# Attention in a two-layer mixer and MoE kernel: the values are held in the array, the probabilities stream, two heads share the columns, and the output stays transposed

## What is computed

```
# windowed heads, latent queries: a band of +-128 latent keys, all context keys, one sink
p = softmax(concat([s_loc, s_ctx, s_sink]));  o = p[:, :-1] @ v
# latent-attention heads: all latent and context keys
p = softmax(s * (64 + 32) ** -0.5);           o = p @ v
# context queries (first layer only): context keys alone
y = concat([o_swa, o_gdn, o_mla]) @ w_out
x = x + g1 * rms_norm(y)
h2 = rms_norm(x) * (1 + sc2) + sh2
```

## Time and profile before

| | us |
|---|---|
| median of 3 runs | 3174.64 |
| lowest and highest | 3173.73, 3174.68 |
| profiled execution: its own time | 3172.74 |
| its span (first to last instruction) | 3170.9 |
| mean granted TensorE clock | 0.948 of full |

### The profile page before, as it was taken

How to read it: one execution, slowest core, us unless ns; L and a number is a source line. 1 busy time by engine, 2 the same in 40 slices (tenths; PEclk the granted TensorE clock), 3 DMA queues, 4 the chain that set the end, 5 groups by cost and what they waited for, 6 DMA issues and landing times. The chain is left out here.

```text
span 3170.9 us, 57994 instructions
## 1 busy us (share of the span) xinstructions
PE 2841.6 (90%) x20700; PEld 1444.7 (46%) x20701; DVE 1516.1 (48%) x2944; ACT 840.6 (27%) x1553; POOL 949.0 (30%) x928
## 2 busy tenths in 40 slices
PE   6998897988999999999977998988989898978895
PEld 3654665874543333333323554667854332222232
DVE  2432653864554444444436443636745544433345
ACT  2231543112212222222225232441122222211222
POOL 0020003521035555555531020006231544433440
PEclk8999998999999999999989999999989999988998
DMA  6100530013348999899949200420134699999955
GB/s 245 62 19 8 186 138 21 4 70 130 146 165 295 367 363 369 319 401 394 364 178 374 95 30 8 159 69 3 35 133 170 249 410 414 406 408 413 408 202 244
DMA packets 129436, 671.63 MB, mean 212 GB/s; under 512 B 38296, under 2 KB 56344, under 8 KB 87392
## 3 DMA queue, kind: packets, MB, share of 16 engines
q1 hardware_dynamic: 86400, 569.34, 46.0%
q0 software_dynamic: 38528, 84.02, 7.2%
q10 hardware_dynamic: 4320, 15.73, 1.2%
HBM read 619.64 MB, written 84.93 MB: 222 GB/s over the span
## 5 line engine op out<-in xcount | busy, mean ns | idle before, releaser
L2325 PE MATMUL psum<-arena 128*64 x1792 | 821.0, 612 | 77.1 <-DVE arena L2419 77.1
L2327 PE MATMUL psum<-arena 128*64 128x512 f32 x1792 | 821.0, 612 | 0.0
L2288 POOL DMA_INDIRECT arena<-h,arena x456 | 521.9, 1145 | 410.0 <-DVE arena L1593 285.6
L2325 PEld LDWEIGHTS psum<-arena 128*64 128x64 f32 x1792 | 242.9, 141 | 566.4 <-issue 566.4
L822 PE MATMUL psum<-arena 128*128 128x480 f32 (+3 forms) x1088 | 405.3, 530 | 16.0 <-PEq L167 8.0
L2347 PE MATMUL psum<-arena 128*64 x896 | 407.7, 598 | 13.2 <-DVE arena L2426 13.2
L2349 PE MATMUL psum<-arena 128*64 128x512 f32 x896 | 407.7, 598 | 0.0
L822 PEld LDWEIGHTS psum<-arena 128*128 128x128 f32 x1088 | 209.3, 196 | 190.6 <-issue 178.2
L2375 ACT ACTIVATE arena<-psum 128x256 f32<-128x256 f32 x112 | 42.9, 383 | 901.5 <-PE psum L2327 901.5
L2347 PEld LDWEIGHTS psum<-arena 128*64 128x64 f32 x896 | 123.7, 138 | 271.7 <-issue 271.7
L2327 PEld LDWEIGHTS psum<-arena 128*64 128x64 f32 x1792 | 242.9, 141 | 0.0
(11 more groups left out here) (360 smaller groups left out, 3987.0 us busy)
## 6 DMA issues: line engine op xcount, KB each, us to landing
arena<-in_w_gu SPq DMA_DIRECT2D x130, 2048.0 KB, 16.6
arena<-in_w_dn SPq DMA_DIRECT2D x130, 1024.0 KB, 13.8
arena<-in_ada SPq DMA_DIRECT2D x24, 2048.0 KB, 8.5
arena<-y_routed SPq DMA_DIRECT2D x40, 1024.0 KB, 14.4
arena<-in_w_gdn SPq DMA_DIRECT2D x6, 1536.0 KB, 11.1
arena<-in_w_out SPq DMA_DIRECT2D x2, 4096.0 KB, 14.9
arena<-in_w_tok SPq DMA_DIRECT2D x4, 1920.0 KB, 7.8
arena<-h,arena POOLq DMA_INDIRECT x464, 7.9
```

Source lines behind the costliest of these rows:

```text
L2288: nc.gpsimd.indirect_dma_start(xg[:, u % 2, b], None, h2_quads, bass.IndirectOffsetOnAxis(ap=idx[:, u, b:b + 1], axis=0), bounds_check=QUA ...
L2325: nc.tensor.matmul(psum[half(0), 2 + r, :], xT[:, r, rows_of(k, 0)], W[:, bass.ds(at + k * 2 * DE, 2 * DE)], start=(k == 0), stop=(k == DK ...
L2327: last = nc.tensor.matmul(psum[half(1), 2 + r, :], xT[:, r, rows_of(k, 1)], late_gu[:, k * 2 * DE:(k + 1) * 2 * DE], start=(k == 0), stop= ...
```

## The change

The attention stage is rewritten; the merge follows from its new output.

- Units are ordered by *pairs* of heads: for each pair and query tile, first one head, then the other. Each SWA pair takes a head of either key group; MLA heads pair up in order.
- POOL, which had nothing to do here, multiplies E by the reciprocal of the sum (in place, one instruction to a unit, 256 to 768 columns) before it is turned. E gets 4 buffers instead of 2.
- `turn` runs two units behind the scores (LAG) and now waits for POOL and for the copy of the unit before.
- `values` runs once for 4 units (two pairs): each key tile's 64 value columns are the weights, 128 columns of ET stream; one head of a pair writes PSUM partitions 0 to 63, the other 64 to 127, and the two alternate. Results are head width by queries.
- DVE's four scaled copies of 64 columns become one plain copy of 256 columns to `catT`. Its old `write` per unit is gone.
- `catT` goes to HBM in 5 stores a layer instead of 10. The rows of `w_out` are permuted on the host to the new order of heads.
- In the merge the attention part loads straight into `cT`; only the 3 GDN blocks are turned and copied. As `cT` has two buffers, `load(i)` gets one more wait: until `project(i-2)` is done. The gate's DMA is still the third of `load_cat`.

```diff
-            for h in range(SWA_H + MH):
+            for m, pair in enumerate(PAIRS):
                 for i in range(nq):
+                    for h in pair:
...
+            LAG, RING, GROUP = 2, 4, 4
...
+                    @block.gpsimd
+                    def _(pool):
+                        for u in range(NU):
+                            w = width(units[u])
+                            pool.wait_ge(normed, u + 1)
+                            nc.gpsimd.tensor_scalar(E[:, u % RING, 0:w], E[:, u % RING, 0:w], den[:, u % 4:u % 4 + 1], None, ALU.mult).then_inc(scaled, 1)
...
                         def turn(u):
-                            pe.wait_ge(exp_done, u + 1)
+                            pe.wait_ge(scaled, u + 1)
+                            if u:
+                                pe.wait_ge(et_done, u)
...
-                        def values(u):
+                        def values(g):
+                            pe.wait_ge(et_done, GROUP * (g + 1))
...
+                                for c, kt in enumerate(keys):
+                                    for x, ((h, i, swa, _, _), r) in enumerate(two):
+                                        v = vb[:, kt, ...] if swa else mv[:, kt, h - SWA_H, :]
+                                        last = nc.tensor.matmul(outs(g)[64 * x:64 * x + 64, p * P:(p + 1) * P], v, ET[:, r, c * P:(c + 1) * P],
...
-                            if u:
-                                values(u - 1)
-                            turn(u)
+                            if u >= GROUP + LAG and (u - LAG) % GROUP == 0:
+                                values((u - LAG) // GROUP - 1)
+                            if u >= LAG:
+                                turn(u - LAG)
...
+                        def write(g):
+                            m, i = 2 * g // nq, 2 * g % nq
+                            dve.wait_ge(pv_done, g + 1)
+                            nc.vector.tensor_copy(catT[:, m, i * P:(i + 2) * P], outs(g)).then_inc(out_done, 1)
...
+        def load_cat(sp, i, cT, sz, c_in):
+            for a, b, at in ((0, NBAND, 0), (NBAND, len(PAIRS), NBAND + GH // 2)):
+                sp.dma_start(cT[:, i % 2, ...], catT_dram[a:b, :, i * P:(i + 1) * P]...).then_inc(c_in[i % 2], 16)
             sp.dma_start(sz[:, i % 2], gate_dram[i * P:(i + 1) * P, :]).then_inc(c_in[i % 2], 16)
...
                             if i >= 2:
                                 sp.wait_ge(turned_a, i - 1)
-                                load_cat(sp, i, ct, sz, c_in)
+                                sp.wait_ge(y_prod, i - 1)
+                                load_cat(sp, i, cT, sz, c_in)
...
-                            for k in range(DK):
+                            for k in range(GH // 2):
...
                             pe.wait_ge(cT_ready, i + 1)
+                            pe.wait_ge(c_in[i % 2], 48 * (i // 2) + 48)
```

More of the change, by code:

```diff
@@ L38 @@
 Z_A = 96
+PAIRS = [(j, SWA_H // SWA_KV + j) for j in range(SWA_H // SWA_KV)] + [(SWA_H + 2 * j, SWA_H + 2 * j + 1) for j in range(MH // 2)]
+NBAND = SWA_H // 2
 TOKC = [W_VB + SWA_KV * HD + KVR + MROPE, SWA_H * HD + Z_A, GH * HD - Z_A + QR]
@@ L1025, in _ @@
                         score(0)
-                        for u in range(NU):
+                        for u in range(NU + LAG):
                             n, at = u // EVERY, u % EVERY
@@ L1086, in _ @@
                             bias(u)
-                            if u >= 2:
-                                write(u - 2)
                             if u >= 1:
                                 norm(u - 1)
-                        if NU >= 2:
-                            write(NU - 2)
+                            if u > GROUP + LAG and (u - LAG - 1) % GROUP == 0:
+                                write((u - LAG - 1) // GROUP - 1)
                         norm(NU - 1)
-                        write(NU - 1)
+                        for g in range((NU - 1 - LAG - 1) // GROUP, NU // GROUP):
+                            write(g)
                     @block.scalar
@@ L1112, in _, with take_row @@
                             nc.scalar.copy(kz[64 * g:64 * g + 64, g], skT[64 * g:64 * g + 64, :]).then_inc(kz_ready, 1)
-                        for u in range(min(2, NU)):
+                        def take_row(m):
+                            act.wait_ge(mod_prod, m + 1)
+                            if m:
+                                act.wait_ge(mod_turned, m)
+                            nc.scalar.copy(row[:, :], psum[:, MOD, :]).then_inc(row_ready, 1)
+                        for u in range(LAG + 1):
+                            if u == 2:
+                                take_row(0)
                             exps(u)
@@ L1778, in take_cat @@
                                 act.wait_ge(y_prod, i - 1)
[L1779 removed]
+                            nc.scalar.copy(cT[:, i % 2, NBAND * P:(NBAND + GH // 2) * P], psum[:, 0, 0:GH * HD]).then_inc(cT_ready, 1)
                         def square_y(i):
@@ L2810 @@
     uq = I["mla_w_uq"]
+    head = [h if h < SWA_H else GH + h for pair in PAIRS for h in pair]
+    heads = head[:2 * NBAND] + list(range(SWA_H, SWA_H + GH)) + head[2 * NBAND:]
+    rows_out = (_np.array(heads)[:, None] * HD + _np.arange(HD)[None, :]).reshape(-1)
     arrays = {
```

110 lines of the change are left out of this document (49 added, 61 removed).

## The result

The changed kernel took 3191.66 us (median of 5 runs, 3188.41 to 3195.41) against 3173.73 us (5 runs, 3173.09 to 3174.68): the ratio is 1.0055, 95% interval 1.0043 to 1.0068. That is 18 us slower, outside the forecast's range of 3142 to 3186. The profiled execution is the slowest of the five, 3195.41 with a span of 3193.6 us.

A forecast was written before the change was run, and what follows sets the result against it. The prediction took PE to set the attention stages' pace, values passes being held by their 128-column weight loads. Attention -39 and merge +30 gave -9, so 3165 us; the range leaving out two in ten was 3142 to 3186.

The forecast's parts named there:

- Values on column halves, -51 us: Attention values: two heads' halves run side by side, a key tile costing 0.107 us instead of 0.22, over 448 tiles.
- The change of shape, +6: Attention: TensorE going from halves to the full array and back costs 0.24 us, paid 25 times, +6 us.
- VectorE, ScalarE and the score buffers, +5: Attention: scores wait for exponentials two units back, 16 us if nothing is absorbed, 0 if all is; +5 taken.
- GpSimd, 0: Attention: POOL's multiplication at 1.1 to 2.2 ns a column, 1.5 taken, is hidden up to about 2.6; costs nothing.
- Attention, -39: Both attention stages together: -51 + 6 + 5 + 1 = -39 us, with bounds -56 and -20.
- The merge, +30: Merge of both layers: -1, +21 for five late gates and +10 for the clock, +30 us, bounds 14 to 45.
- The landing: Merge: the gate's load, issued when the projection ends, lands in 3.2 us; the row read gave 3.6.
- The clock: Merge: idle gaps halve TensorE's granted clock for the work behind, 2 us in each of five places, +10.
- Five transposes less: Merge: fewer transposes and copied columns per tile save almost nothing, as PE waits for ACT's copy anyway; -1 us.
- Rival 1: Merge hides its loads better: gate lands in 2.6 us, clock doesn't fall, merge costs 14; 3149 us, chance 0.20.
- Rival 2: Attention paced by DVE and the two score buffers, gaining only 20 us; 3185 us, slower, chance 0.16.
- rivals 3 and 4: Attention: POOL becomes the bound (3203 us), or halves don't overlap at 128 columns (3215 us); together 0.05.

The follow-up runs named there:

- 7: Kernel 1 with the two heads of a pair worked one after the other, each on its column half, instead of alternating by key tile: 3174.97 us.
- 11: Kernel 1 with the values gathered in pairs of units instead of fours, 50 changes to halves and back instead of 25: 3149.04 us.
- 8: Kernel 1 with GpSimd multiplying only 2 columns of each unit, every wait kept, values wrong: 3196.17 us; first layer's attention 171.0 us in both.
- 9: Kernel 1 with GpSimd scaling the first 512 columns of units of 5 and 6 key tiles and VectorE the rest: 3154.04 us.
- 5: The changed kernel with the gate's DMA issued first of the three and counted on semaphores of its own, all three still waiting for the projection: 3171.68 us.
- Run 3: The changed kernel with seven matmuls nobody reads ahead of each GDN turn that waits for the gate, keeping TensorE busy: 3175.61 us.
- 12: Kernel 1 with the gates' DMAs one tile further ahead, plus two matmuls nobody reads ahead of each tile's logits: 3136.27 us.
- kernel 1: The changed kernel with the gate's DMA no longer waiting for the projection and on its own semaphores; the attention loads still wait: 3149.56 us.
- 4: The changed kernel with the gate's DMA issued first of the three of a tile, VectorE still waiting for the count of all three: 3188.77 us.
- 6: The changed kernel with ScalarE's 512 KB store of h issued some 10 us later, behind its work on x: 3184.86 us.

## Why the prediction was wrong, step by step

- **Values on column halves, -51 us: right**, in size and reason. 0.108 us a tile against the forecast 0.107, and a pass whose neighbours are on its own half takes 0.109, as before the change (7): the overlap is the gain. PE's busy time fell by 38 us, though, and not by the 45 of this term and the next; where the other 7 went wasn't traced.
- **The change of shape, +6: near in size (25 x 0.19 = 5), wrong in place.** It is busy time of PE, but twice as many changes leave the time as it was (11).
- **VectorE, ScalarE and the score buffers, +5: right only as a sum**; PE's gaps grew by 4 us. The scores now wait 14 us for the exponentials two units back (7.7 and 0.9 in the first layer, 5.5 in the second), near the 16 of the forecast's worst case. Against that the wait for ACT's copy, which was to stay, fell from 21 to 10 us. The two errors cancel.
- **GpSimd, 0: right in the sum, wrong in the price.** 2.5 ns a column and 0.28 us lay outside the bounds, since both neighbouring rows were of another kind of instruction. At 640 columns that is 1.88 us, 2.9 ns a column with the fixed part, over the 2.6 up to which the forecast called it hidden, and 768 columns took 2.20 us where its sign said under 1.7; it was hidden all the same (8, 9). That point was too cautious.
- **Attention, -39: -35.** The sum stood, in part by the errors above.
- **The merge, +30: +49. This is the step that failed**, and in size only: the five places, the wait and its releaser were the forecast's. Two terms of it were too small. *The landing*, 3.2 us taken, was 5.2: the row of 3.6 was read as an upper case, since a 512 KB load stood ahead of it, but the new issue moment falls together with the 512 KB store of h and the load of x, and the gate is third; in later places it took up to 6.0. With 2.3 us and no issue ahead of it (5) the kernel is 20 us faster. *The clock*, 5 x 2 = 10 taken, was about 17: the projections lost 1.84, 1.3, 2.6, 2.4 and 1.8 us, 9.9 together, and the forecast had priced the logits at their full-clock 1.8 us; at 1.2 GHz they lose 1.5 more, four times, and the turns 0.3, five times. Run 3 returns 16 by the medians and 20 by the stages. The forecast's own row of the half clock had a slow small piece as well as a slow projection in it, and 2.6 us for them; "I take 2 each" took away what the row showed. The gap of the place shown adds up to 3.9 + 2.0 + 1.5 + 0.3 = 7.7 against 12.2 - 4.4 = 7.8 measured. Its signs missed with it: the turns wait 7.0 to 8.0 us and not 5, and the projections start 28 us apart and not 24.
- **The bounds of the merge, 14 to 45,** are not what their own terms give: -1 + 21, five times 0.6 less or 2.8 more for the landing, and 0 or 5 x 2.6 for the clock make 17 and 47. Even 47, with the longest landing seen, ends short of 49, because the half clock in the logits, 1.5 us in four places, is in no term.
- **Five transposes less, "almost nothing":** they leave PE idle 0.5 us longer ahead of the logits, and some of the projections behind that take 15.5 to 15.65 us instead of 13.95. That is the 4 us which 12 gave back.
- **The rest, 0: +8.5 in the profiled pair.** By the medians, -35 and +49 leave +4. With 12 a similar amount came and went in stretches that nobody changed, so it is no part of the change that these runs can show.
- **Rivals.** Rival 1 (a merge that hides better) has the time of kernel 1, 3149.6 us against the 3149 worked out for it, by luck: there the merge costs 7 us and not 14, attention gives 35 and not 39, and the mechanism is another, the wait moved and not shortened. Rival 2's wait for the score buffers did come, but attention gained 35 us and not 20; rivals 3 and 4 did not come about: GpSimd cost nothing, the halves overlap.

## What to carry to other kernels

When a buffer gets a second user, put the new wait in front of the one transfer that needs it: here a load of another tensor stood behind it in the same function, and that alone turned a gain of 24 us into a loss of 18. Price a wait on TensorE by what it does to the clock of the work behind it too: the small pieces right behind it as well as the long one. And price a transfer that is newly issued at a certain moment by what else is issued at that moment, and by which semaphore counts it: landing early is worth nothing while the count includes a later one.

## What the runs showed of the hardware that was not expected

- The third of three loads on one queue landed in 5.2 to 6.0 us, the first two in 2.3 to 2.7, whether the gate or the attention output was third (4, changed kernel); without a 512 KB store beside them the third took 3.9 (6). In kernel 5 the second took 4.0 and the third 4.7 in the first gap, 2.8 and 5.3 in the next.
- Pauses of 1.14 to 1.23 us ahead of the logits were followed by a projection of 13.95 us with a granted clock of 1.00, and by one of 15.65 us whose first 3.5 us had 0.55 (kernel 1). A pause of 1.47 us was followed by 13.95 in the kernel before and by 15.50 in kernel 1, so its length alone doesn't decide. Filling the pauses with matmuls that nobody reads brought all to 13.95 (12).
- A pass of 64 columns that streams 128 takes 0.109 us when its neighbours use the same half and 0.054 when they use the other (7, changed kernel); with 128 columns and a stream of 64 it took 0.11. Where a head on one half ends and one on the other half begins, their passes overlap though they stand one after the other in the program.
- GpSimd's multiplication by a scalar of its own for each partition costs 2.5 ns a column and 0.28 us; for 2 columns it took 0.29 us (8).
